# Expert phase of a two-block transformer kernel in eight half phases, rows handed over in twos, top-k rounds spread between the row sums, first gathers inside the query product

## The reference

```python
def peer_sublayer(h, w_query, sub_keys, u, v):      # PEER_BLOCK 128, 8 heads, top 16
    def block(hb):                                  # 128 tokens, twice
        q = (hb @ w_query).reshape(128, 8, 2, 128)
        s = jnp.einsum('thpc,hpnc->thpn', q, sub_keys)
        top_s, top_i = lax.top_k(s, 16)
        cand_s = top_s[:, :, 0, :, None] + top_s[:, :, 1, None, :]     # 16 x 16 candidates
        cand_i = top_i[:, :, 0, :, None] * 128 + top_i[:, :, 1, None, :]
        best_s, best_j = lax.top_k(cand_s, 16)
        idx = take_along_axis(cand_i, best_j)       # 8 heads x 16 = 128 experts a token
        g = jax.nn.softmax(best_s, axis=-1)
        a = jax.nn.gelu(jnp.einsum('thkd,td->thk', u[idx], hb))
        return jnp.einsum('thk,thkd->td', g * a, v[idx])
```

## Time and profile before

| | |
|---|---|
| median of 3 runs | 3643.81 us (3643.04 to 3649.52) |
| profiled execution, device time | 3643.92 us |
| its span in the trace | 3642.1 us, 42655 instructions |
| share of the span busy | PE 71%, POOL 70%, DVE 44%, ACT 31% |
| gathers (queue q0) | 536.97 MB |

### The profile page before, as it was taken

One profiled execution on the slowest core, in us unless ns is written; L12 is line 12 of the kernel. 1 busy time (PEld: TensorE's weight loads), 2 busy tenths in 40 slices (PEclk: granted clock), 3 DMA queues, 4 the chain that ended last, 5 costly groups with the idle time before them and its releaser, 6 DMA issues.

```text
span 3642.1 us, 42655 instructions
## 1 busy us (share of the span) xinstructions
PE 2595.8 (71%) x15849; PEld 2029.6 (56%) x15849; DVE 1596.8 (44%) x2160; ACT 1132.2 (31%) x2121; POOL 2532.0 (70%) x1835
## 2 busy tenths in 40 slices
PE   7996596978999999979997988600038780003887
PEld 6875485768978998869985667600013330001333
DVE  4002457123200121020004412999999549996444
ACT  5442423454444444444436744300000000000000
POOL 7887505857989998978874057778865548886452
PEclk9998797999999999989998589855568985556889
DMA  5665300535655665546652044599989999999997
GB/s 180 180 201 151 102 3 2 168 116 154 186 172 188 182 186 170 188 124 177 175 153 87 1 132 148 211 411 427 427 362 427 427 427 427 427 427 427 427 427 327
DMA packets 239026, 867.95 MB, mean 238 GB/s; under 512 B 18498, under 2 KB 20676, under 8 KB 171908
## 3 DMA queue, kind: packets, MB, share of 16 engines
q0 software_dynamic: 73776, 536.97, 35.0%
q1 hardware_dynamic: 162550, 316.11, 28.4%
q10 hardware_dynamic: 2540, 12.75, 1.2%
HBM read 860.24 MB, written 2.10 MB: 237 GB/s over the span
## 4 chain that ended last, share of the span: by engine, by line
PE 52%; DVE 17%; POOL 14%; DMA 8%; issue 6%; ACT 2%; DVEq 0%; POOLq 0%; SPq 0%; ACTq 0%
PE acc L1602 20%; PE acc L1597 19%; DVE zone L1517 8%; DMA zone<-in_peer_v,zone 7%; PE acc L2051 7%; POOL zone L665 5%; POOL w_lo L549 4%; POOL lasting L665 4%; PE acc L1693 2%; PE acc L1870 1%; DVE x_lo L1125 1%; PE acc L1857 1%; DVE zone L1269 1%; PE acc L1950 0%; DVE zone L1400 0%
## 5 line engine op out<-in xcount | busy, mean ns | idle before, releaser
L549 POOL TENSOR_TENSOR w_lo<-lasting,w_hi 128x512 fp32r<-128x512 f32 (+1 forms) x1184 | 1574.7, 1347 | 474.4 <-ACT w_hi L698 441.0
L2051 PE MATMUL acc<-zone,lasting 128*128 128x512 f32 x1024 | 510.0, 662 | 787.4 <-DMA zone<-in_peer_v,zone 787.4
L698 ACT ACTIVATE w_hi<-lasting 128x512 fp32r<-128x512 f32 (+1 forms) x1184 | 744.0, 633 | 956.2 <-PE acc L1597 500.6
L2051 PEld LDWEIGHTS acc<-zone,lasting 128*128 128x128 f32 x1024 | 214.8, 213 | 1081.9 <-issue 1081.9
L1543 DVE SCALAR_TENSOR_TENSOR lasting<-lasting,zone 128x2048 f32<-128x2048 f32 x128 | 301.0, 2351 | 241.3 <-DMA lasting<-in_peer_v,zone 233.3
L1602 PE MATMUL acc<-x_hi,w_hi 128*128 128x256 f32 (+1 forms) x2112 | 344.0, 285 | 16.7 <-DVE x_lo L1125 10.4
L1602 PE MATMUL acc<-x_lo,w_hi 128*128 128x256 f32 (+1 forms) x2112 | 341.3, 284 | 0.0
L1602 PE MATMUL acc<-x_hi,w_lo 128*128 128x256 f32 (+1 forms) x2112 | 340.1, 283 | 0.0
L665 POOL DMA_INDIRECT zone<-in_peer_v,zone x128 | 181.5, 1418 | 211.4 <-PE acc L2051 179.4
L1517 DVE CUSTOM_DVE_ANT_0 zone<-lasting,zone 128x2048 f32<-128x2048 f32 x128 | 293.4, 2292 | 27.6 <-DMA lasting<-in_peer_u,zone 14.1
L1602 PEld LDWEIGHTS acc<-x_hi,w_hi 128*128 128x128 f32 x2112 | 291.5, 190 | 18.7 <-DVE x_lo L1125 11.2
(11 more groups left out here) (371 smaller groups left out, 3305.4 us busy)
## 6 DMA issues: line engine op xcount, KB each, us to landing
lasting<-in_w_in SPq DMA_DIRECT2D x200, 512.0 KB, 3.6
lasting<-in_w_up SPq DMA_DIRECT2D x128, 512.0 KB, 3.8
lasting<-in_w_down SPq DMA_DIRECT2D x128, 512.0 KB, 3.9
lasting<-in_w_mix_out SPq DMA_DIRECT2D x32, 512.0 KB, 3.7
lasting<-in_w_out SPq DMA_DIRECT2D x32, 512.0 KB, 3.6
lasting<-in_peer_w_query SPq DMA_DIRECT2D x32, 512.0 KB, 3.9
lasting<-in_w_kv_cross SPq DMA_DIRECT2D x16, 512.0 KB, 3.9
lasting<-in_w_q_cross SPq DMA_DIRECT2D x8, 512.0 KB, 3.3
```

The lines of the kernel that those rows point to most:

```text
L549: pool.tensor_tensor(w_lo[:, k, 0:width], ring[:, slot, s % SLOT_SLABS, 0:width], w_hi[:, k, 0:width].bitcast(FP32), ALU.subtract).then_in ...
L698: act.activation(w_hi[:, s % PARTS, 0:width], ring[:, slot, s % SLOT_SLABS, 0:width], ACT.Copy).then_inc(hi_ready, 1)
L2051: last = pe.matmul(bank(4 * t + c), diag[:, n // 2, j], rows_buf[4 * n + j][:, c * CHUNK:(c + 1) * CHUNK], start=i == 0 and n == 1 and j = ...
```

## The change

Each tile's 128 rows are now done as two halves of 64: `u` rows of half 0, `v` rows of half 0, and so on, eight phases of four rounds of 16 rows. The 16 buffers form eight pairs in place of four groups of four; pairs 0, 2, 4, 6 go to PE and 1, 3, 5, 7 to DVE in a `v` round. DVE chooses only heads for the first half (`choose(0, 0)`, `choose(0, 1)`) before the first dot products; the other six `choose` stand after the first and second `v` round of a half, two in each of the first three halves. The gates, the Gelu and the Exp are done per half. POOL issues four gathers between the last slabs of the query product, into buffers that lie over tensors already dead there; then it waits for PE to finish the product, and only before pair 6 for `s_sp` 4. The banks of tile 0 are added after the third `v` round of tile 1's first half, and the output is written in four DMAs of 256 KB a tile, each after its add.

```diff
-        spots = [n * D for n in range(4)] + [base + (3 + n) * D for n in range(4)] + [X0 + n * D for n in range(4)]
-        spots += [base + 2 * D, base + 7 * D, base + 8 * D, z]
+        spots = [base + n * D for n in (2, 5, 7, 8)] + [n * D for n in range(4)] + [X0 + n * D for n in range(4)]
+        spots += [z] + [base + n * D for n in (3, 4, 6)]
...
-        junk = scores[:, 0]
-        diag = at(diag_at, 2, 4, P)
+        junk = hot.rearrange("p a b -> p (a b)")
+        diag = at(diag_at, 4, 2, P)
+        PAIRS_OF_ROWS, HALF_ROWS = 8, P // 2
+        ROUNDS = HALF_ROWS // (2 * PAIRS_OF_ROWS)
...
+        dots_round, sums_round = (lambda hx, i: 2 * hx * ROUNDS + i), (lambda hx, i: (2 * hx + 1) * ROUNDS + i)
+        BY_PE, BY_DVE = range(0, PAIRS_OF_ROWS, 2), range(1, PAIRS_OF_ROWS, 2)
...
             for t in range(TILES):
-                sp.wait_ge(s_hb, TILES + 4 * (t + 1))
-                sp.dma_start(out[0, t * P:(t + 1) * P, :], h[:, t]).then_inc(s_out, 16)
+                for c in range(4):
+                    cols = slice(c * CHUNK, (c + 1) * CHUNK)
+                    sp.wait_ge(s_hb, TILES + 4 * t + c + 1)
+                    sp.dma_start(out[0, t * P:(t + 1) * P, cols], h[:, t, cols]).then_inc(s_out, 16)
...
+                                if (c, s) in after:
+                                    after[c, s]()
...
-            for k in range(4):
-                pool.sem_inc(rows_used[k], 1)
-            pool.wait_ge(s_sp, 4)
...
+            def gather(phase, i, n, k):
+                (hx, table), rnd = EXPERT_PHASES[phase], phase * ROUNDS + i
+                if n == 0 and k == 0 and i % 2 == 0:
+                    pool.wait_ge(s_ix0, 2 * hx + i // 2 + 1)
+                if k == 0 and rnd:
+                    pool.wait_ge(rows_used[n], rnd)
...
+            early = [(n, k) for n in range(2) for k in range(2)]
+            rests("query", after={(3, 7 + 2 * e): lambda n=n, k=k: gather(0, 0, n, k) for e, (n, k) in enumerate(early)})
+            chunk_done(pool, G["query"], 3)
+            for phase in range(len(EXPERT_PHASES)):
+                for i in range(ROUNDS):
+                    for n in range(PAIRS_OF_ROWS):
+                        if phase == 0 and i == 0 and n < 2:
+                            continue
+                        if phase == 0 and i == 0 and n == 6:
+                            pool.wait_ge(s_sp, 4)
+                        for k in range(2):
+                            gather(phase, i, n, k)
...
+            for hx in range(2 * TILES):
+                act.wait_ge(s_dot, hx + 1)
+                part = dots[:, hx // 2, half_slice(hx)]
+                act.activation(part, part, ACT.Gelu).then_inc(s_gelu, 1)
+                act.wait_ge(s_coefs, hx + 1)
+                for i in range(ROUNDS):
+                    for n in BY_PE:
+                        if i:
+                            act.wait_ge(rows_used[n], sums_round(hx, i))
+                        for k in range(2):
+                            slot = row_of(hx, i, n, k)
+                            last = act.activation(diag[:, n // 2, k], ident, ACT.Copy, scale=coef[:, hx // 2, slot:slot + 1])
+                        last.then_inc(s_diag, 1)
+                    if i == 2 and hx + 1 < 2 * TILES:
+                        exp_gates(hx + 1)
...
+            def coefs(hx):
+                t, part = hx // 2, half_slice(hx)
+                dve.nop().then_inc(s_dot, 1)
+                gates(hx)
+                dve.wait_ge(s_gelu, hx + 1)
+                step(TT(coef[:, t, part], coef[:, t, part], dots[:, t, part], ALU.mult))
+                dve.nop().then_inc(s_coefs, 1)
...
+            def add_sums(t):
+                for n in BY_PE:
+                    dve.wait_ge(rows_used[n], sums_round(2 * t + 1, ROUNDS - 1) + 1)
                 for c in range(4):
                     cols = h[:, t, c * CHUNK:(c + 1) * CHUNK]
                     TT(cols, bank(4 * t + c), cols, ALU.add).then_inc(s_hb, 1)
+            for c in range(2):
+                dve.wait_ge(s_sc, c + 1)
+                choose(0, c)
+            for hx in range(2 * TILES):
+                dot_products(hx)
+                coefs(hx)
+                for i in range(ROUNDS):
+                    weigh_rows(hx, i)
+                    if i < 2 and hx + 1 < 2 * TILES:
+                        t, c = (hx + 1) // 2, (hx + 1) % 2 * 2 + i
+                        if t == 0:
+                            dve.wait_ge(s_sc, c + 1)
+                        choose(t, c)
+                    if i == 2 and hx == 2:
+                        add_sums(0)
+            add_sums(1)
...
-                                                 start=i == 0 and n == 1 and j == 0, stop=i == 7 and n == 3 and j == 3)
+                                                 start=hx % 2 == 0 and i == 0 and n == 0 and k == 0,
+                                                 stop=hx % 2 == 1 and i == ROUNDS - 1 and n == 6 and k == 1)
```

More of the change, by code:

```diff
@@ L536, in block_diagonal, with rests @@
                 keep(v, [[b, P // b], [0, b]], b - 1, -1)
-            def rests(*names):
+            def rests(*names, after={}):
                 for name in names:
@@ L1530, in coefs, with gates @@
-            def coefs(t):
+            def gates(hx):
+                t, hs = hx // 2, slice(4 * (hx % 2), 4 * (hx % 2) + 4)
+                dve.wait_ge(s_be, hx + 1)
+                step(RED(esum[:, t, hs], cw(t)[:, hs], AX, ALU.add))
+                step(dve.reciprocal(esum[:, t, hs], esum[:, t, hs]))
+                step(TT(cw(t)[:, hs], cw(t)[:, hs], esum[:, t, hs].unsqueeze(2).to_broadcast([P, 4, E_TOP]), ALU.mult))
+            def coefs(hx):
+                t, part = hx // 2, half_slice(hx)
@@ L1545, in weigh_rows @@
                             last.then_inc(rows_used[n], 1)
                         dve.drain()
-            for c in range(4):
-                dve.wait_ge(s_sc, c + 1)
-                choose(0, c)
-            gates(0)
-            dot_products(0, range(8))
-            coefs(0)
-            for i in range(8):
-                if i < 4:
-                    choose(1, i)
-                weigh_rows(0, i)
-            gates(1)
-            dot_products(1, range(8))
-            coefs(1)
-            for i in range(8):
-                weigh_rows(1, i)
```

108 lines of the change are left out of this document (43 added, 65 removed).

## The result

The changed kernel takes 3617.6 us (median of four runs, 3609.08 to 3618.14), against 3644.84 us for the kernel before in the same session (3643.04 to 3649.52). The medians are 27 us apart; the ratio over all runs is 0.9919, with a 95% interval of [0.9905, 0.9932]. The profiled run took 3617.24 us with a span of 3615.4 us, where the prediction has 3612.6 and 3610.8.

The account below looks back on a forecast made before the run. The prediction took the expert phase to be bound by its stream of 537 MB of gathers. Its terms, -9.9 + 1.5 - 1.4 - 12.8 + 2.4 - 11.1 = -31.3 us, gave span 3610.8 and device time 3612.6 us, range 3604 to 3627.

Parts of the forecast that it names:

- What bounds the phase: In the expert phase, 537 MB of gathers bound the time, at 2.472 us a row by landings.
- Early gathers: Four gathers between the last query-product slabs move rows while the stream is empty, 4 x 2.47 = 9.9 us off.
- the fifth gather: First gather behind the query product: issued near 2338.3, +1.5 us against the first gather before; bounds -3.7 and +6.
- rival (b): At the query product's end, POOL's delay pushes the next gather back by what four early rows gain: +8.4 us, 3621; chance 0.05.
- Stands: Pauses of the gather stream at 2375 (1.4 us) and 2695, ahead of the first `v` round (12.8 us), both go.
- Output of tile 0: Its 1 MB moves from the end into the full gather stream: one row's worth, +2.4 us; bounds 0 and 3.9.
- The tail: From last landing to end of span: 9.8 us in place of 20.9, so -11.1; bounds 8.6 and 12.
- Last landing: The last gathered row at the end of the expert phase was to land near 3601.
- Rival (a): Stands of 1 to 4 us at four seams and six chooses: about 13 us, time 3626; chance 0.09.
- Rival (c): In `v` rounds PE stays at half clock, a pair takes 13.8 us: slower, about 3825; chance 0.05.
- Rival (d): Nothing to measure: some unseen wait takes both seams and the tail's gain, about 3640; chance 0.05.

## Why the prediction was right, and which term was off

- **What bounds the phase.** Right. Share 1.01 from 2350 to 3590, and in eight of the ten kernels one price of a row, 2.476 to 2.477 us, where the prediction has 2.472; one had stands, and the one with spread gathers lost 3.4 us.
- **Early gathers, -9.9.** Right as a number of rows: three rows fewer after the output's 1 MB is counted. What they bring in the end is less, see the fifth gather and rival (b).
- **The fifth gather, +1.5, bounds -3.7 and +6.** Here is the miss: +4.0 measured, the issue 2.8 us later than before (40.01 against 37.23) and 1.3 us longer (2.30 against 1.04). The mechanism was the one written down, DVE's dot products holding up POOL, but two sizes were off. The hold-up of POOL is in the sum at 2.3 us, all of it on the slabs; it was 3.5, of which 2.1 on the fourth gather, taken at its short price, and 1.4 on the slabs. Since the undelayed end was 0.6 us sooner than reckoned, POOL's last slab came only 0.6 us later than the prediction has it. The larger part, 2.0 us, lies behind that slab: PE ended the product 3.4 us behind it, at 2341.3, where the sum has 1.4. A fall of the clock is not in the sum at all: after its pause of 4.11 us PE worked at a granted clock of 0.50, that is 1.2 GHz, from 2336.75 to 2339.50, which cost 1.5 us. The other 0.5 us is there in the run with the wait for the product as well (1.9 us behind the last slab). The wait on DVE took away the 3.5 and the 1.5.
- **Stands, -1.4 and -12.8.** Right in size: gone, and they come back, at 18.5 us, with the old order of chooses alone. The reason given for the second was only half of it. The prediction puts it on the place of the choose behind `weigh_rows` and its 16 us of margin; the runs show that the place in the round changes nothing, and that the earlier start of the dot products, which the prediction credits with the first stand alone, removes both.
- **Output of tile 0, +2.4.** Right; moving it out gave 2.3.
- **The tail, 9.8 in place of 20.9.** 10.6, so 0.8 too low. DVE's part was right (4.78 + 0.26 + 2.48). From the last issue at 3612.3 to the end of the span are 3.1 us, where 2.4 stood: a piece of 256 KB takes 2.3 to 2.7 us from issue to landing, not the 2.1 that was got by subtraction. The prediction finds its row's 3.9 us for 1 MB in agreement with a fixed 2.0 us plus the bytes; with the 2.4 us that it takes for the bytes that makes 4.4, so they agree only to half a microsecond.
- **Last landing** near 3601.0, measured 3604.7: 2.5 from the start, 0.7 from the common point, 0.4 from the price of a row, together 3.6 of the 3.8.
- **Rival (a), new stands.** Fell: no stretch of 10 us between 2350 and 3590 is under share 1.00. It was near, though: in the kernel with spread gathers POOL's issues fell behind the stream, and 3.1 us were lost within the first 70. POOL's 2.41 us a gather, which the prediction reads from one step, is the shortest step; under dot products the steps run up to 2.84 us in the changed kernel and to 3.23 in that one.
- **Rival (b), early gathers bring nothing.** Fell by its own terms: the start came 4.0 us later than before, not the 9.9 that four rows bring. But measured against the same kernel without early gathers it is near: 9.9 brought and 7.5 pushed back (42.31 against 34.85). What keeps the total good is the removed wait for the key scores, 3.4 us, which the prediction counts (-3.7 when nothing is late) and which needs no early gather.
- **Rival (c), PE at half clock in the `v` rounds.** Fell: no pair held up the stream. But the low clock came back more often than in the first passes of a phase. Of the 64 pairs of the changed kernel 40 take 7.03 to 7.11 us, at full clock. The other 24 take 8.5 to 10.15 us, two of them over the 9.8 us of landings, with slow first passes. After a pause of 2.6 to 2.9 us the clock had fallen in 15 pairs and not in 14; the last two pairs show both:

```profile
3590.19 7.11 PE L2085 MATMUL acc<-lasting 128*128 128x512 f32 x16 [2.69 <-DMA lasting<-in_peer_v,zone]
3599.96 8.62 PE L2085 MATMUL acc<-zone,lasting 128*128 128x512 f32 x16 [2.67 <-DMA zone<-in_peer_v,zone]
...
3599.96:3602.00 2.04, 2.04 (x3) 1.01 (x4) 0.00 (x0) 0.00 (x0) 0.00 (x0) 0.50 0.07 28
```

  The Trainium skill, "TensorE: Matmul & The Clock Gate", section "HAM oscillation", has bursts of matmuls of about 2 us with waits of 3 to 5 us between them fall back to the low clock in every burst; here bursts of 7.1 us with pauses of 2.6 to 2.9 us fell back in about half, at 1.4 to 1.7 us each. The runs do not show what decides between the two.
- **Rival (d).** Fell with the above.

## What to carry over

When an engine finishes early what it used to finish late, look at what it will start at once and which other engine's work or queue it will disturb: here the first dot products, moved 37 us forward, held up four POOL instructions and through them PE, its clock and the stream, and one wait on the engine that had nothing to gain from being early gave 4.5 us back. In a phase bound by a stream, count in rows: the time from the end of the first open issue to the last landing is rows times one price, so that each edit is worth its rows, its shift of the start, its stands and its tail, and here, but for the kernel with spread gathers, these add up to a few tenths of a microsecond. A consumer only slightly faster than the stream carries a late start for hundreds of microseconds, and the next piece of other work on it then stops the stream: look for the stand's cause where it fell behind, not where the stream stopped.

## What the hardware showed

- **A gather's issue on POOL** takes 0.93 to 1.35 us when DVE is idle or in small instructions, mostly 2.1 under a dot product, and up to 3.05 when a dot product has just started (3.05 with one 0.06 us old, 2.97 with one 0.14 us old). When the gather began 0.02 us ahead of the dot product or in the same hundredth of a microsecond, it took 0.95 us. The Trainium skill, "SBUF — State Buffer", section "Who interferes with whom", has two-input VectorE instructions take only the read interface of the ports shared with GpSimd, and infers that generating descriptors needs the write interface, so that it would not be held up. The measurement disagrees, and it decides: the same fourth gather took 3.05 with the dot product beside it and 0.95 without.
- **TensorE's clock** fell after a pause of 4.1 us within dense work (two kernels, 4.11 and 4.09: groups of 1.23 to 1.05 us instead of 0.64, granted 0.50 in the first), and did not after pauses of 1.78 and 1.59 us with work between (granted 1.00). After the pauses of 2.6 to 2.9 us between pairs it fell in 15 cases of 29.

```profile
2336.75:2339.50 2.75, 2.75 (x13) 2.75 (x14) 1.11 (x1) 0.00 (x0) 1.18 (x1) 0.50 0.38 158
```

- **One DMA engine's worth trails.** The engines as a whole move a row of 1.0486 MB in 2.456 us at 427 GB/s, yet a row costs 2.477. The 0.02 us between them are some 10 us over the phase, and something of that size shows at the end, in bandwidth over 40 slices of 0.64 us from 3590 on in the changed kernel:

```profile
GB/s 429 441 454 429 416 429 366 290 265 189 101 38 25 25 25 25 38 25 25 25 25 25 0 0 0 0 0 0 0 0 0 0 60 369 391 328 366 101 0 0
```

From about 3597 to 3604 only 25 GB/s flow, about one sixteenth of the full rate of 427, so about one engine's worth of 16. That it is a single engine, and what makes it late, was not tried.
